# mLSTM decay weights: running maxima spread over the partitions through HBM instead of by matmuls, and a compact scratch for the relative bias

## The reference

```
m_t   = running maximum of a up to t (and 0)          # one row of 256 numbers per head and direction
w[s,t] = exp(a[s] - m_t)  for s <= t, else 0          # the decay weights
score = (k_s . q_t) * w[s,t] ;  h_t = sum_s score v_s / max(|sum_s score|, exp(-(b_t + m_t)))
```

## Time and profile before

| | |
|---|---|
| median of 3 runs | 966.62 us |
| the profiled execution's own time | 966.37 us |
| its span, first to last instruction | 964.6 us |
| mean granted clock of TensorE | 0.979 |
| TensorE (PE) busy | 912.1 us, 95% |
| VectorE (DVE) busy | 557.2 us, 58% |
| ScalarE (ACT) busy | 452.5 us, 47% |
| GpSimd (POOL) busy | 36.9 us, 4% |
| DMA queue q0, issued by GpSimd | 1664 packets, 6.82 MB, 4.3% of the 16 engines' span |
| chain that ended last | PE 86%, DVE 5%, DMA 4%, ACT 3% |

### The profile page before, as it was taken

One profiled execution on the slowest core, in us unless ns is written; L12 is line 12 of the kernel. 1 busy time (PEld: TensorE's weight loads), 2 busy tenths in 40 slices (PEclk: granted clock), 3 DMA queues, 4 the chain that ended last, 5 costly groups with the idle time before them and its releaser, 6 DMA issues.

```text
span 964.6 us, 14223 instructions
## 1 busy us (share of the span) xinstructions
PE 912.1 (95%) x5740; PEld 809.1 (84%) x5740; DVE 557.2 (58%) x718; ACT 452.5 (47%) x581; POOL 36.9 (4%) x83
## 2 busy tenths in 40 slices
PE   6999998599999998899999999999998899999997
PEld 6987777599999986767899999988996799999996
DVE  4696674455455555783745555565666645554554
ACT  5365453444444445583544444445555444333432
POOL 1000011000000002001100000001000010000000
PEclk9899999799999998999999999999999899999999
DMA  9353259756655442317456555555531536556541
GB/s 300 120 175 106 93 135 109 256 184 199 186 195 193 158 142 97 121 45 258 156 181 194 193 188 201 175 175 175 175 132 49 170 131 194 200 174 197 173 152 44
DMA packets 97671, 156.85 MB, mean 163 GB/s; under 512 B 4015, under 2 KB 72236, under 8 KB 97628
## 3 DMA queue, kind: packets, MB, share of 16 engines
q1 hardware_dynamic: 94908, 149.37, 47.3%
q0 software_dynamic: 1664, 6.82, 4.3%
q10 hardware_dynamic: 1056, 0.07, 0.1%
HBM read 152.06 MB, written 4.19 MB: 162 GB/s over the span
## 4 chain that ended last, share of the span: by engine, by line
PE 86%; DVE 5%; DMA 4%; ACT 3%; issue 1%; POOL 0%; DVEq 0%; ACTq 0%; SPq 0%
PE psum L1569 27%; PE psum L1570 26%; PE psum L1571 26%; DMA raw<-in_ffn_w 3%; DVE h_lo L1053 1%; DVE w_lo L1028 1%; PE psum L1604 1%; PE psum L1986 1%; DVE arena L1408 1%; ACT w_hi L637 1%; ACT h_hi L664 1%; PE psum L1957 1%; ACT arena L881 1%; PE psum L1780 1%; PE psum L2021 1%
## 5 line engine op out<-in xcount | busy, mean ns | idle before, releaser
L1569 PE MATMUL psum<-h_hi,w_hi 128*128 128x256 f32 x1072 | 308.6, 288 | 19.0 <-DVE w_lo L1028 11.9
L1570 PE MATMUL psum<-h_lo,w_hi 128*128 128x256 f32 x1072 | 306.4, 286 | 0.0
L1571 PE MATMUL psum<-h_hi,w_lo 128*128 128x256 f32 x1072 | 306.3, 286 | 0.0
L1028 DVE TENSOR_TENSOR w_lo<-raw,w_hi 128x2048 fp32r<-128x2048 f32 (+2 forms) x74 | 163.9, 2221 | 120.0 <-ACT w_hi L637 119.7
L1569 PEld LDWEIGHTS psum<-h_hi,w_hi 128*128 128x128 f32 x1072 | 209.0, 195 | 23.5 <-DVE w_lo L1028 12.3
L1043 DVE TENSOR_TENSOR w_lo<-raw,w_hi 128x2048 fp32r<-128x2048 f32 x66 | 151.3, 2292 | 105.0 <-ACT w_hi L655 105.0
L1570 PEld LDWEIGHTS psum<-h_lo,w_hi 128*128 128x128 f32 x1072 | 209.0, 195 | 1.5
L1571 PEld LDWEIGHTS psum<-h_hi,w_lo 128*128 128x128 f32 x1072 | 208.8, 195 | 0.0
L637 ACT ACTIVATE w_hi<-raw 128x2048 fp32r<-128x2048 f32 (+2 forms) x74 | 136.1, 1844 | 102.6 <-PE psum L1571 84.4
L655 ACT ACTIVATE w_hi<-raw 128x2048 fp32r<-128x2048 f32 x66 | 125.9, 1908 | 69.5 <-PE psum L1571 69.5
L1569 PE MATMUL psum<-w_hi,g_hi 128*128 128x512 f32 x368 | 143.8, 391 | 0.0
(11 more groups left out here) (233 smaller groups left out, 777.2 us busy)
## 6 DMA issues: line engine op xcount, KB each, us to landing
raw<-in_ffn_w SPq DMA_DIRECT2D x64, 1024.0 KB, 5.2
raw<-in_ab_w_in SPq DMA_DIRECT2D x12, 1024.0 KB, 5.5
raw<-in_w_qkv SPq DMA_DIRECT2D x12, 1024.0 KB, 5.1
raw<-in_w_gate SPq DMA_DIRECT2D x11, 1024.0 KB, 5.3
raw<-in_w_up SPq DMA_DIRECT2D x11, 1024.0 KB, 5.3
raw<-in_w_down SPq DMA_DIRECT2D x11, 1024.0 KB, 4.9
raw<-in_ab_w_out SPq DMA_DIRECT2D x4, 1024.0 KB, 4.9
raw<-in_c_w_out SPq DMA_DIRECT2D x4, 1024.0 KB, 5.0
```

Source lines behind the costliest of these rows:

```text
L1028: ins = dve.tensor_tensor(dst, src, high, ALU.subtract)
L1569: pe.matmul(dst, stat[0], mov[0], start=first, stop=False)
L1570: pe.matmul(dst, stat[0], mov[1], start=False, stop=False)
L1571: return pe.matmul(dst, stat[1], mov[0], start=False, stop=last)
```

## The change

1. **m through HBM.** TensorE's `spread_m` is gone, and with it the tile `mask`, its three GpSimd instructions, and `nsel` with its VectorE instruction. GpSimd waits for `rows_ready` and stores `m_row` in four small DMAs to `m_scratch` in HBM (4 heads x 2 directions x 3 blocks of 128). When they have landed it loads, for each direction, 1536 bytes per partition and head, the same on all partitions, into `decay[0]` (all of `g_act`) and `decay[1]` (a new piece of the arena), 768 KB each. It then masks in place: two `affine_select` a direction, each over 4 heads x 128 targets.
2. **decay_of** reads and writes `decay[back]` in SBUF with scale -1, waits for the mask of its direction only, and its order on ScalarE changes: units 0 to 3, then `hi` of piece 10, then units 4 to 7, then `hi` of piece 11. All 8 units have a place of their own, so nothing waits for `g_ready` any more.
3. **Compact relative bias.** `rel_scratch` holds one copy a head (24 KB). `rel_ext` is built in the other order, the load into `bias2` takes row p from offset p, and `bias_max` reads `bias2` backwards.

```diff
+            pool.wait_ge(rows_ready, 1)
+            m_out = m_dram.ap()
+            for b, back, t0 in ((0, slice(0, 2), 0), (2, slice(0, 2), P), (1, slice(0, 1), P), (1, slice(1, 2), 0)):
+                pool.dma_start(m_out[:, back, b, :], m_row[0:A_H, back, t0:t0 + P]).then_inc(m_stored, 16)
+            pool.wait_ge(vecs_turned, 2)
+            pool.wait_ge(m_stored, 64)
+            for back in range(2):
+                pool.dma_start(decay[back], bass.AP(m_dram, back * 3 * P, [[0, P], [6 * P, A_H], [1, 3 * P]]))\
+                    .then_inc(m_spread[back], 16)
+            for back in range(2):
+                pool.wait_ge(m_spread[back], 16)
+                for b in (0, 2):
+                    own = decay[back][:, :, b * P:(b + 1) * P]
+                    ins = pool.affine_select(out=own, in_=own, compare_op=ALU.is_ge, fill=-NEG, base=0,
+                                             pattern=[[0, A_H], [(1, -1)[back], P]],
+                                             channel_multiplier=(-1, 1)[back])
+                ins.then_inc(m_masked, 1)
             rms("vb")
             rms("ha")
...
-            pool.dma_start(rel_dram.ap(), rel_ext[:, :].unsqueeze(1).to_broadcast([H2, P, EXT])).then_inc(rel_stored, 16)
+            pool.dma_start(rel_dram.ap(), rel_ext[:, :]).then_inc(rel_stored, 16)
...
-                    pool.dma_start(bias2[:, :, :], bass.AP(rel_dram, P - 1, [[EXT - 1, P], [P * EXT, H2], [1, S]]))\
+                    pool.dma_start(bias2[:, :, :], bass.AP(rel_dram, 0, [[1, P], [EXT, H2], [1, S]]))\
...
             def decay_of(u):
-                act.wait_ge(spread, u + 1)
-                if u >= 2:
-                    act.wait_ge(g_ready, u - 1)
...
+                act.wait_ge(m_masked, back + 1)
+                w = decay[back][:, h, :]
...
-            decay_of(0)
-            decay_of(1)
+            for u in range(4):
+                decay_of(u)
             hi(P_VB + 1 + RING)
-            decay_of(2)
+            for u in range(4, 2 * A_H):
+                decay_of(u)
             hi(P_U + RING)
-            decay_of(3)
-            decay_of(4)
...
-                for qb, (c0, c1, k0) in enumerate(((0, P, P), (P, 3 * P, 0))):
+                for qb, (c0, c1, last) in enumerate(((0, P, P - 1), (P, 3 * P, S - 1))):
...
-                                                   bias2[:, h, k0:S], -1.0, -NEG, ALU.add, ALU.min,
+                                                   bias2[:, h, last::-1], -1.0, -NEG, ALU.add, ALU.min,
...
             def unit_step(u):
-                if u + 2 < 2 * A_H:
-                    spread_m(u + 2)
```

More of the change, by code:

```diff
@@ L153, in build @@
         ident = sb("ident", [P, P])
-        mask = sb("mask", [P, 2, P])
         vecs = sb("vecs", [VECS, P])
@@ L225, in build @@
         ones_row = ca(S)
-        nsel = ca(A_H, P)
         a_col = ca(TB, 8)
@@ L325, in build @@
         vbn_ready = sem("vbn_ready")
-        spread = sem("spread")
+        m_stored = sem("m_stored")
+        m_spread = [sem(f"m_spread{back}") for back in range(2)]
+        m_masked = sem("m_masked")
         w_ready = sem("w_ready")
@@ L578, in _ @@
             rms("ab1")
[L581 to L585, removed]
             for i in range(HALF):
@@ L612, in _ @@
                     pool.wait_ge(bias_loaded, 16)
-                    pool.memset(bias2[0:CHUNK, :, P + CHUNK:S], NEG).then_inc(bias_ready, 1)
+                    pool.memset(bias2[0:CHUNK, :, 0:S - P - CHUNK], NEG).then_inc(bias_ready, 1)
                 rms(name)
@@ L758, in decay_of @@
                 h, back = u // 2, u % 2
[L759 to L763 removed]
+                act.wait_ge(m_masked, back + 1)
+                w = decay[back][:, h, :]
                 at = back * A_H + h
[L765 to L766 removed]
+                for s0, (c0, c1) in enumerate([((0, 256), (256, 384)), ((0, 128), (128, 384))][back]):
+                    ins = act.activation(w[:, c0:c1], w[:, c0:c1], ACT.Exp, bias=a_col[:, s0, at:at + 1], scale=-1.0)
                 ins.then_inc(w_ready, 1)
[L770 to L771 removed]
+            for u in range(4):
+                decay_of(u)
             hi(P_VB + 1 + RING)
[L773 removed]
+            for u in range(4, 2 * A_H):
+                decay_of(u)
             hi(P_U + RING)
[L775 to L776 removed]
             act.wait_ge(piece_used, P_U + 2)
@@ L1202, in weigh @@
                 src = bank(2 + h % 2)
-                w = decay[:, u % 2, :, :].rearrange("p b t -> p (b t)")
+                w = decay[back][:, h, :]
                 dst = score[:, u % 2, :, :].rearrange("p b t -> p (b t)")
-                for c0, c1 in [((0, 256), (384, 512)), ((0, 128), (256, 512))][back]:
+                for c0, c1, w0 in [((0, 256, 0), (384, 512, 256)), ((0, 128, 0), (256, 512, 128))][back]:
                     ins = dve.scalar_tensor_tensor(out=dst[:, c0:c1], in0=src[:, c0:c1], scalar=float(A_D) ** -0.5,
-                                                   in1=w[:, c0:c1], op0=ALU.mult, op1=ALU.mult)
+                                                   in1=w[:, w0:w0 + c1 - c0], op0=ALU.mult, op1=ALU.mult)
                 ins.then_inc(g_ready, 1)
@@ L1735, in _ @@
             moving(P_VB, (0, 1))
[L1737 to L1754, removed]
             def head_scores(h):
@@ L1809, in _ @@
                         head_scores(0)
-                    if j == 0 and i == 1:
-                        spread_m(0)
-                        spread_m(1)
                     if j == 0 and i >= 2:
```

21 lines of the change are left out of this document (9 added, 12 removed).

## The result

The changed kernel takes 942.40 us (median of 4 runs, 942.21 to 945.79) against 966.53 us of the kernel before beside it (966.12 to 968.50): ratio 0.9755, 95% interval 0.9729 to 0.9780. The prediction was 944.0, range 940.5 to 949.5. The profiled execution took 942.31 us, its span is 940.5 us.

The account below looks back on a forecast made before the run. TensorE, busy 95% of the span, was taken as the bound, with VectorE near enough to take over in the mLSTM stage. 966.4 - 8.5 - 14.0 = 943.9 us, stated as 944, range 940.5 to 949.5.

Parts of the forecast that it names:

- Compact scratch, -13.96: First feed-forward block: with the store cut to 24 KB it takes as long as the second, 13.96 us less.
- slower rival: Second block: short reads out of 24 KB starve its weight pieces; 983 us at a 60 us transfer; chance 0.03.
- Load out of 24 KB, 0: Load into bias2: same 2048 rows of 1 KB, 9.6 us before, only GpSimd waits for it; cost 0.
- hot spot: Slower rival's fear: one place of the HBM serves the 2048 short reads out of 24 KB one after the other.
- Backward read, 0: VectorE reading bias2 backwards: cost 0, with 16 us as the upper bound at half speed.
- Small operations, 0: nsel, mask, consts: one VectorE and three GpSimd operations go, all before 31 us and beside TensorE's work; 0.
- spread_m, -8.5: mLSTM stage: 15.0 us of TensorE work goes, 8.5 us arrive at the turn; bounds 5.8 to 10.4.
- four waits of TensorE: mLSTM stage, new order: TensorE waits 2.2 us for the first weigh, then 0.6, 2.2 and 1.2 at VectorE's pace.
- m and the masks: Before the first exp: m landed at 60 and 63, masks of 0.63 us done by 69, each blocking VectorE throughout.
- the clock falls in the mLSTM stage: Rival: short waits around 91 us lower TensorE's clock, costing at most 3.4 us, 2.4 if partly hidden; 946.5 us; chance 0.20.
- 6.5 of 15 us: mLSTM stage: the part of the 15.0 us saved on TensorE that goes to VectorE and the masks.

Follow-up runs that it names:

- e5: The changed kernel plus a further 3 MB store out of a tile of zeros on all 128 partitions; 944.46 us (943.86 to 945.53).
- e3: The changed kernel without GpSimd's four masks (other output), a tiny memset giving the signal instead; 942.89 us (942.04 to 945.15).
- e7: The changed kernel with each pair of masks done twice, same output; 944.05 us (943.26 to 944.84).
- e8: The changed kernel with GpSimd masking only after the last of VectorE's four convolutions; 942.71 us (941.30 to 944.50).
- e11: The changed kernel plus a further 4.5 MB store out of the 16 partitions of the bias rows; 973.73 us, ratio 1.0056 to the kernel before.

## Why the prediction was right

Step by step, in its own terms:

- *Compact scratch, -13.96:* -13.95 in the profile, and 14.1 in the time when done alone (13.96 in the block; a fall of the clock behind the mLSTM stage and the missing one at the last turn about cancel). The cause is shown, not only the place: with another store of the same kind the stall is back, in the size that the transfer's length gives. The prediction's sentence for its slower rival, that each further us of a transfer beyond 35.2 costs one more, measured 0.97.
- *Load out of 24 KB, 0:* 9.9 us for 9.6, waited for by GpSimd alone. Nothing of the hot spot.
- *Backward read, 0:* the `bias_max` operations, 16 short and 16 long ones, last 281 to 289 and 419 to 420 ns, for 283 to 289 and 419 to 423 before.
- *Small operations, 0:* the operation behind the last scan began at 46.57 us, at 46.72 before.
- *spread_m, -8.5:* the turn came at 112.21, forecast 112.4; OA at 96.67, forecast 96.9. The forecast had four waits of TensorE, 2.2 + 0.6 + 2.2 + 1.2 = 6.2 us; measured are 2.18 + 1.07 + 0.95 = 4.20, all for `weigh`. The 0.6 and half of the second 2.2 are missing because the clock had fallen and TensorE was slower; without the fall (e5) the four are 2.17, 0.48, 1.92 and 0.95. So the rows carried over to the new order.
- *m and the masks:* the parts were less exact than the sum. The four small stores landed by 51.7, 4.1 us from the first issue and not 6; the two loads took 7.1 and 8.3 us side by side, where the prediction took about 3 for each. Its own terms (47.4 + 6 + 3, and 3 more) give 56.4 and 59.4 for the landings, not the 60 and 63 that it states. That the masks ran at 58.9 to 62.4 was near these by luck; forecast was 60 to 69, and nothing waited for them. A mask took 0.71 to 0.75 us beside VectorE and 0.62 alone, forecast 0.63. But VectorE lost 0.37 us for each, where the prediction took the mask's whole length: 1.5 for all four, 1.8 expected from the three ahead of the last convolution. That the two hold each other up is shown (e3, e7, e8); that one waits for the whole of the other's operation is seen for GpSimd behind a long subtraction (2.55 us), not for VectorE behind a mask. The prediction had the two exclude each other for the whole operation; VectorE's 0.37 us for a mask of 0.62 is below that. The two errors, more masks ahead and less for each, cancel: luck.
- *The clock:* the rival "the clock falls in the mLSTM stage" had 0.20, and the fall came: 0.93 and 0.73 in 75 to 85 us, 3.4 us at the lower level. It came behind the first wait, not around 91 us, and was half as long as the 6.8 us that the rival took from the last turn, so at most 1.7 us could be lost. Its price was wrong. The prediction gave it 2.4 us with a part hidden; all of it was hidden, since TensorE caught up before its wait at 91.94, and the turn is where it is without a fall (e5). It was the stage's new slack that paid.
- *Not foreseen:* the 1.8 us behind the second block, and the 0.4 lost between the blocks. Both go with the clock: before, e3 and e8 need 118.2 to 118.3 us between the blocks, the others 118.4 to 118.8. Without these the ledger is 22.7 us, forecast 22.5.

What stays open: what decides at which of its stretches of short waits the clock falls, and so the last 1.5 us of any version.

## What to carry to other kernels

A transfer that runs beside a stream of weights costs nothing up to a certain length (here it was free at 18.1 us, and by the line it begins to cost at 21), since the pieces loaded ahead carry the work, and from there about one us for each us. Find the length from the list of DMA issues, and a sister stretch of the program without it as the yardstick. Source a large store from all partitions; 16 of them gave a third of the rate. When work is taken from the bounding engine, lay the new order out by hand with the measured durations of the next engine: it told the turn within 0.2 us for this change and within 0.1 us for one reordering after it (a second it missed by over 1 us), and it showed that 6.5 of 15 us would not arrive.

## What the runs showed of the hardware

- 3 MB in pieces of 1536 B from SBUF to HBM: 12.3 us out of 128 partitions, 35.1 and 35.2 out of 16; 1.5 MB out of 16 in 18.1.
- While the store out of 16 partitions ran (e11, 129 to 158 us), all transfers together moved 110 GB/s with the DMA engines 0.97 busy.
- 2 MB in rows of 1 KB read out of 24 KB of HBM take 9.9 us, out of 3 MB 9.6; two loads of 768 KB, each out of 6 KB, took 7.1 and 8.3 side by side. No hot spot is seen.
- The two-input VectorE operation of `bias_max` takes as long with one input read backwards as with both read forwards (281 to 289 and 419 to 420 ns, for 283 to 289 and 419 to 423).
- A mask of 0.62 us on GpSimd costs the two-input VectorE operations beside it 0.34 to 0.37 us; a mask issued 0.24 us into a VectorE subtraction of 2.29 us took 2.55.
- The same stretch of code at the last turn, TensorE busy 7.0 to 7.3 of 10 us, has a fall of the clock or not; in 13 of 13 profiles it has one just where the mLSTM stage and its turn, some 650 us earlier, had none.
- A fall of 3.4 us at half clock delayed the turn by 0.15 us at most where TensorE had waits for VectorE ahead (112.21 with it, 112.18 without), and cost 1.0 to 1.6 us elsewhere between 90 and 130 us.
